# Modulation rows gathered in one accumulation bank per group of blocks, with twelve blocks in the opening

## The reference

```python
cond_lat = jax.nn.silu(c)[:, None, :]
cond_ctx = jax.nn.silu(c_ctx)[None, None, :]
for i in range(DEPTH):
    sh1, sc1, g1, sh2, sc2, g2 = jnp.split(cond_lat @ w_ada[i] + b_ada[i], 6, axis=-1)
    csh1, csc1, cg1, csh2, csc2, cg2 = jnp.split(cond_ctx @ w_ada[i] + b_ada[i], 6, axis=-1)
    h_lat = modulate(rms_norm(x, norm_gain[i, 0]), sh1, sc1)
    ...                                   # mixer: Fourier for i = 0, differential attention for i = 1
    x = x + g1 * o_lat
    x = x + g2 * swiglu(modulate(rms_norm(x, norm_gain[i, 1]), sh2, sc2), ffn_w_in[i], ffn_w_out[i])
```

## Time and profile before

| what | value |
|---|---|
| time, median of 3 runs | 2476.74 us (2475.94 to 2478.11) |
| profiled execution | 2477.43 us |
| its span, first to last instruction | 2475.3 us |
| PE busy | 2406.6 us, 97% of the span |
| DVE busy | 1295.9 us, 52% |
| ACT busy | 879.2 us, 36% |
| POOL busy | 374.7 us, 15% |
| granted PE clock, mean | 0.991 |

### The profile page before, as it was taken

One profiled execution on the slowest core, in us unless ns is written; L12 is line 12 of the kernel. 1 busy time (PEld: TensorE's weight loads), 2 busy tenths in 40 slices (PEclk: granted clock), 3 DMA queues, 4 the chain that ended last, 5 costly groups with the idle time before them and its releaser, 6 DMA issues.

```text
span 2475.3 us, 34693 instructions
## 1 busy us (share of the span) xinstructions
PE 2406.6 (97%) x14346; PEld 2015.3 (81%) x14346; DVE 1295.9 (52%) x2101; ACT 879.2 (36%) x1499; POOL 374.7 (15%) x301
## 2 busy tenths in 40 slices
PE   8999999999999999999999999999999999999999
PEld 6778888888887777656888887988989878877788
DVE  3765635543535776775333336465565445554433
ACT  4332111211224544434222124454544334444422
POOL 0210000000014444501000001234333410000000
PEclk9999999999999999999999999999999999999999
DMA  9734334334311111012333332222122121121222
GB/s 324 206 97 120 121 111 126 120 119 119 107 64 35 51 52 35 35 51 69 98 90 102 99 89 87 67 69 65 56 69 86 52 69 52 52 69 52 79 92 111
DMA packets 252744, 220.79 MB, mean 89 GB/s; under 512 B 7480, under 2 KB 243443, under 8 KB 252204
## 3 DMA queue, kind: packets, MB, share of 16 engines
q1 hardware_dynamic: 249072, 217.92, 28.6%
q10 hardware_dynamic: 3260, 0.58, 0.1%
q0 software_dynamic: 256, 0.07, 0.0%
HBM read 214.26 MB, written 6.29 MB: 89 GB/s over the span
## 4 chain that ended last, share of the span: by engine, by line
PE 60%; ACT 3%; DVE 3%; issue 2%; POOL 1%; DVEq 0%; ACTq 0%; POOLq 0%
PE two L685 10%; PE bank L1354 5%; PE bank L1545 4%; PE bank L685 4%; PE bank L1350 3%; PE bank L1331 3%; PE two L1285 3%; PE bank L1526 2%; PE bank L1051 2%; PE two L1156 2%; PE bank L1182 2%; PE two L1565 2%; PE bank L1021 1%; PE bank L1033 1%; PE two L1443 1%
## 5 line engine op out<-in xcount | busy, mean ns | idle before, releaser
L2560 DVE TENSOR_TENSOR wL<-ring,wH 128x512 fp32r<-128x512 f32 x224 | 182.9, 831 | 226.9 <-ACT wH L1832 226.7
L1823 ACT ACTIVATE wH<-ring 128x2048 fp32r<-128x2048 f32 (+1 forms) x80 | 149.1, 1864 | 272.1 <-PE bank L690 73.4
L2549 DVE TENSOR_TENSOR wL<-ring,wH 128x2048 fp32r<-128x2048 f32 (+1 forms) x80 | 179.0, 2237 | 82.2 <-ACT wH L1823 82.0
L685 PE MATMUL two<-h1H,wH 128*128 128x512 f32 x496 | 195.5, 394 | 0.0
L685 PE MATMUL two<-h1H,wL 128*128 128x512 f32 x496 | 193.5, 390 | 0.0
L685 PE MATMUL two<-h1L,wH 128*128 128x512 f32 x496 | 193.4, 390 | 0.0
L1832 ACT ACTIVATE wH<-ring 128x512 fp32r<-128x512 f32 x224 | 133.6, 623 | 60.3 <-PE bank L1331 22.5
L1901 ACT ACTIVATE gateS<-two 128x512 f32<-128x512 f32 x44 | 26.3, 598 | 330.5 <-PE bank L690 142.0
L2653 DVE SCALAR_TENSOR_TENSOR xT<-two,ada,xT 128x512 f32<-128x512 f32 (+1 forms) x48 | 30.6, 680 | 186.3 <-PE bank L690 66.3
L3196 POOL TENSOR_TENSOR rstd<-rstd,sq 128x768 f32<-128x768 f32 (+1 forms) x15 | 30.4, 2027 | 610.6 <-ACT sq L1859 609.6
L1354 PE MATMUL bank<-unH,wH 128*128 128x272 f32 (+1 forms) x368 | 111.9, 304 | 1.3 <-issue 0.8
(11 more groups left out here) (642 smaller groups left out, 6962.1 us busy)
## 6 DMA issues: line engine op xcount, KB each, us to landing
ring<-in_ffn_w_in SPq DMA_DIRECT2D x88, 512.0 KB, 5.2
ring<-in_w_in SPq DMA_DIRECT2D x40, 1024.0 KB, 5.0
ring<-in_w_ada SPq DMA_DIRECT2D x32, 1024.0 KB, 5.3
ring<-in_ffn_w_out SPq DMA_DIRECT2D x16, 1024.0 KB, 5.1
early<-in_w_ada SPq DMA_DIRECT2D x12, 1024.0 KB, 12.2
ring<-in_diff_w_in SPq DMA_DIRECT2D x12, 1024.0 KB, 5.2
ring<-in_w_proj_ssd SPq DMA_DIRECT2D x8, 1024.0 KB, 4.9
ring<-in_ffn_w_out SPq DMA_DIRECT2D x8, 768.0 KB, 4.6
```

Of the source, the lines that this page charges most:

```text
L685: m = nc.tensor.matmul(bank[3 * s + half], w, r[:, 0:LAT], start=i == 0, stop=i == n - 1)
L1823: nc.scalar.activation(hi, raw, ACT.Copy).then_inc(w_hi, 1)
L2549: nc.vector.tensor_tensor(lo, raw, hi.bitcast(F32), ALU.subtract).then_inc(w_lo, 1)
L2560: nc.vector.tensor_tensor(lo, raw, hi.bitcast(F32), ALU.subtract).then_inc(q_lo, 1)
```

## The change

The two ways become one. Blocks are gathered in six groups: blocks 0 to 7, blocks 8 to 11, and of the other 36 (`MORE`) numbers 0 to 7, 8 to 11, 12 to 27 and 28 to 35. All blocks of a group add into one bank: the weight tile is cut from a wider `condz` (62 columns, the two conditions in the middle), so that block j of a group lands in rows 2j and 2j + 1 of each strip. After the last block DVE copies the bank once (`sums_out`), PE collapses it with two products against a selector of 32 columns (`cols_of`), and DVE stores all columns of the group at once (`take_ada`). DVE no longer sums blocks. The opening has 12 blocks instead of 16, the Fourier tiles 8 instead of 4, the feed-forward 28 as before, one after each of units 1 to 28. The loads of the first two Fourier blocks go between the modulation loads, the first directly behind block 7; POOL folds all four, and the first split moves in ACT's and DVE's order.

```diff
-ADA0 = [4, 5, 6, 7, 0, 1, 2, 3] + list(range(8, FRONT))
+ADA0 = list(range(FRONT))
+UNITS0 = sum([[("in", 0, c) for c in range(lo, hi)] + [("down", 0, lo, cb) for cb in range(4)] for lo, hi in GROUPS], [])
+ADA_GROUPS = [[("ada", 0, b) for b in range(8)], [("ada", 0, b) for b in range(8, FRONT)], MORE[0:8], MORE[8:12], MORE[12:28], MORE[28:36]]
+ROWS_AT = {0: [0], 1: [1], 2: [2], 3: [3], 4: [4, 5], 5: [6], 6: [7]}
...
-    plan = [("ada", 0, b) for b in ADA0]
-    plan += [("fnet", 0), ("fnet", 1), ("fnet", 2), MORE[0], ("fnet", 3)] + MORE[1:4]
+    plan = [("ada", 0, b) for b in range(8)] + [("fnet", 0)] + [("ada", 0, b) for b in range(8, FRONT)]
+    plan += [("fnet", 1), ("fnet", 2), MORE[0], ("fnet", 3)] + MORE[1:8]
+    for u, unit in enumerate(UNITS0):
+        plan += [unit] + (MORE[6 + u:7 + u] if u >= 2 else [])
...
             sp.dma_start(wback[:, 0, :], w64raw[8:16, :]).then_inc(s_rev, 16)
-            for n in range(8, N_OF[("fnet", 0)]):
-                stream(n)
             sp.wait_ge(s_rev, 32)
             for n in range(N_OF[("fnet", 0)], len(PLAN)):
...
+            def rows_of(key):
+
+                w = slot(N_OF[key])
+                g = [key in group for group in ADA_GROUPS].index(True)
+                j, last = ADA_GROUPS[g].index(key), key == ADA_GROUPS[g][-1]
+                n = N_OF[key]
+                pe.wait_ge(ring_ready[slot_of(n)], arrived(n))
+                if j == 0 and g < 2:
                     pe.wait_ge(s_cols, 3)
+                elif j == 0:
+                    pe.wait_ge(ada_taken, g)
                 for kc in range(KC):
                     q = 32 * (kc % 4)
+                    m = nc.tensor.matmul(bank[(4, 5, 7, 6, 7, 6)[g]][q:q + 32, 0:256], condz[:, kc, 30 - 2 * j:62 - 2 * j], w[:, kc, :],
+                                         start=j == 0 and kc < 4, stop=last and kc >= 4)
                 m.then_inc(ada_row, 1)
...
+            def cols_of(g):
+
+                pe.wait_ge(ada_ev, g + 1)
                 for h in range(2):
+                    m = nc.tensor.matmul(bank[6 + g % 2 if g < 2 else 7 - g % 2][:, 256 + 32 * h:288 + 32 * h], adacc[:, g % 2, P * h:P * h + P], sel,
                                          start=True, stop=True)
                 m.then_inc(ada_done, 1)
...
             def more_columns(key):
+                u = UNITS0.index(key)
+                for g in (3, 4, 5):
+                    if u == MORE.index(ADA_GROUPS[g][-1]) - 6:
+                        cols_of(g)
+                if 1 <= u < len(MORE) - 7:
+                    rows_of(MORE[7 + u])
...
-                    pe.wait_ge(ada_taken, FRONT + 4)
+                    pe.wait_ge(ada_taken, 3)
...
                 for i in ([], [], [0], [1], [2, 3], [4], [5, 6], [7])[g]:
                     ada_rows(i)
-                    if i:
-                        ada_cols(i - 1)
-            ada_cols(7)
             for kc in range(4):
                 x_turned(kc)
-                ada_rows(8 + kc)
-                if kc:
-                    ada_cols(7 + kc)
+                if kc == 0:
+                    cols_of(0)
+                if kc < 2:
+                    ada_rows(8 + kc)
             for p in range(4):
                 dft_features(p)
-                ada_rows(12 + p)
-                ada_cols(11 + p)
+                if p in (1, 2):
+                    ada_rows(9 + p)
             dft_middle()
-            ada_cols(FRONT - 1)
+            cols_of(1)
...
-            keep_busy(4, 5)
+            keep_busy(2, 5)
...
+            cols_of(2)
...
+            for t in range(9):
+                if t == 5:
+                    split_hi(0)
...
+            def sums_out(g):
+
+                dve.wait_ge(ada_row, sum(len(x) for x in ADA_GROUPS[:g + 1]))
+                if g >= 2:
+                    dve.wait_ge(ada_done, g - 1)
+                nc.vector.tensor_copy(adacc[:, g % 2], bank[(4, 5, 7, 6, 7, 6)[g]][:, 0:256]).then_inc(ada_ev, 1)
...
             def more_sums(key):
+                u = UNITS0.index(key)
+                for g in (3, 4, 5):
+                    if u == MORE.index(ADA_GROUPS[g][-1]) - 7:
+                        sums_out(g)
+                    if u == MORE.index(ADA_GROUPS[g][-1]) - 6:
+                        take_ada(g)
...
             turned_lat(4)
             turned_lat(5)
-            folded_weights()
+            split_lo(0)
             turned_lat(6)
             turned_lat(7)
-            split_lo(0)
             split_lo(1)
...
                     mixed(m)
-                    for j in ROWS_AT.get(m, ()):
-                        strip_out(j)
-                    for j in COLS_AT.get(m, ()):
-                        take_ada(FRONT + j)
+                    if m == 6:
+                        sums_out(2)
                 split_lo(cb + NS)
+            take_ada(2)
             multipliers(1)
...
-            for cb in range(1, 4):
+            for cb in range(4):
                 n = N_OF[("fnet", cb)]
                 w = slot(n)
-                pool.wait_ge(w_sum, 2 * cb)
                 pool.wait_ge(ring_ready[slot_of(n)], arrived(n))
-                pool.wait_ge(w_lo, max(cb - 1, 1))
+                if cb == 0:
+                    pool.wait_ge(f_a, 2 * KC)
+                if cb >= 2:
+                    pool.wait_ge(w_lo, cb - 1)
```

More of the change, by code:

```diff
@@ L30 @@
 EARLY = 24
-FRONT = 16
+FRONT = 12
 NS = 2
@@ L61, in constants @@
         k[:, K_NYQ + 33 * j] = np.cos(a)[:, DH]
-    for c in range(2):
-        k[c::32, K_SEL + c] = 1.0
+    k[:, K_SEL:K_SEL + 32] = i[:, None] % 32 == i[None, 0:32]
     k[2, K_BIAS] = 1.0
@@ L139, in stream_plan @@
 def stream_plan():
-    plan = [("ada", 0, b) for b in ADA0]
-    plan += [("fnet", 0), ("fnet", 1), ("fnet", 2), MORE[0], ("fnet", 3)] + MORE[1:4]
+    plan = [("ada", 0, b) for b in range(8)] + [("fnet", 0)] + [("ada", 0, b) for b in range(8, FRONT)]
+    plan += [("fnet", 1), ("fnet", 2), MORE[0], ("fnet", 3)] + MORE[1:8]
+    for u, unit in enumerate(UNITS0):
+        plan += [unit] + (MORE[6 + u:7 + u] if u >= 2 else [])
     for layer in range(2):
[L144 to L151, removed]
+        if layer:
+            for lo, hi in GROUPS:
+                plan += [("in", 1, c) for c in range(lo, hi)] + [("down", 1, lo, cb) for cb in range(4)]
         if layer == 0:
@@ L714, in ada_rows @@
                 m.then_inc(ada_row, 1)
[L716 to L735, removed]
@@ L743, in strip_cols, with ada_rows @@
                 m.then_inc(ada_done, 1)
[L745 to L750, removed]
-                        o = 4 * h + 2 * c
-                        m = nc.tensor.matmul(bank[6 + j % 2][:, o:o + 2], adacc[:, j % 2, c, P * h:P * h + P], ones[:, 0:2],
-                                             start=True, stop=True)
-                m.then_inc(ada_done, 1)
+            def ada_rows(i):
+                rows_of(("ada", 0, i))
@@ L866, in _ @@
             for _ in range(11):
-                nc.tensor.matmul(bank[7][:, 0:256], condz[:, 0:4, :].rearrange("p c n -> p (c n)"), condz[:].rearrange("p c n -> p (c n)"),
-                                 start=True, stop=True)
+                zeros = condz[:].rearrange("p c n -> p (c n)")
+                nc.tensor.matmul(bank[7][:, 0:256], zeros[:, 0:P], zeros[:, 0:256], start=True, stop=True)
             for g in range(KC):
@@ L988, in _ @@
             ffn(0)
-            pe.wait_ge(ada_taken, 48)
+            pe.wait_ge(ada_taken, 6)
             norm_sums(2, True)
@@ L1768, in _ @@
             act.wait_ge(s_cols, 3)
-            for to in (condz, cond):
-                for j, r in enumerate((ROW_C, ROW_CC)):
-                    nc.scalar.activation(to[:, :, j], colA[:, r:r + 8], ACT.Silu).then_inc(s_cols, 1)
+            for j, r in enumerate((ROW_C, ROW_CC)):
+                nc.scalar.activation(condz[:, :, 30 + j], colA[:, r:r + 8], ACT.Silu).then_inc(s_cols, 1)
             nc.scalar.preload_act_table_set("natural_log_exp_and_others")
@@ new lines, in take_ada @@
+            def take_ada(g):
+                dve.wait_ge(ada_done, g + 1)
+                n, (_, layer, b) = len(ADA_GROUPS[g]), ADA_GROUPS[g][0]
+                src = bank[6 + g % 2 if g < 2 else 7 - g % 2][:, 256:320].rearrange("p (h m) -> p h m", h=2)[:, :, 0:2 * n]
+                src = src.rearrange("p h (j c) -> p j h c", c=2)
+                o = 48 * layer + 2 * b
+                bias = colB[:, o:o + 2 * n].rearrange("p (j h) -> p j h", h=2).unsqueeze(3).broadcast_to([P, n, 2, 2])
+                nc.vector.tensor_tensor(ada[layer][:, 2 * b:2 * b + 2 * n, :].rearrange("p (j h) c -> p j h c", h=2), src, bias, ALU.add) \
+                    .then_inc(ada_taken, 1)
@@ L2440, in more_sums @@
             def more_sums(key):
[L2442 removed]
+                if key not in UNITS0:
                     return
[L2444 to L2468 removed]
@@ L2470, in multipliers @@
+                u = UNITS0.index(key)
[4 more added lines that the diff above has]
+                        take_ada(g)
```

(5 more changed lines are left out.)

147 lines of the change are left out of this document (29 added, 118 removed).

## The result

The changed kernel takes 2508.0 us, median of 4 runs (2504.4 to 2514.2), against 2476.4 (2475.9 to 2478.1) for the kernel before: 1.0129 times as long, interval 1.0115 to 1.0143. It is slower, by 31.6 us; 23.8 were forecast. The median lies 1 us above the forecast range of 2489 to 2507.

The account below looks back on a forecast made before the run. TensorE was taken to bound layer 0's feed-forward, with a serial chain behind the opening. Terms -1.7 + 2.3 + 2.3 + 1.2 + 3.5 + 11.2 + 5.0 = 23.8 us on the 2476.74 median gave 2500.5, range 2489 to 2507.

Parts of the forecast that it names:

- The two stops: Feed-forward units 5 and 21: TensorE stands until VectorE takes the group before, 6.9 and 4.3 us, 11.2 lost.
- Rival D: Units 5 and 21: no stop, take done before PE asks or PE runs past; removes 16.2, leaves 7.6; chance 0.05.
- Half clock behind the stops: Feed-forward units 5 and 21: TensorE's clock at half after each stop, 2.5 us each, 5.0 lost (bounds 0 and 7).
- Blocks in the feed-forward stage: Layer 0's feed-forward: 28 wide blocks on TensorE replace 9 blocks and 19 DVE-summed ones, 34.7 for 31.2, 3.5 us lost.
- Fourier tiles and hand-over: Fourier tiles: eight blocks for four, 2.3 us lost; hand-over to the norm: take behind a weight split, another 2.3 lost.
- Half clock at the norm: Before the norm sums: the hole growing to 3.1 us may halve TensorE's clock, 1.7 if it comes, 1.2 taken.
- The opening: Up to the first Fourier tile: start at 96.0 instead of 97.66, 1.7 us won (bounds 3.9 won, 0.9 lost).
- Rival B: Opening: loads run at stream rate once released, block 8 at 61.2, first tile at 88.2, total 2492.7 us; chance 0.14.
- Rival C: Opening held longer by half clock or later Fourier weights: first tile at 98.5 to 101, total 2503 to 2506; chance 0.08.
- Everything behind it is one chain, so the sum needs four pieces: Whole kernel: only opening, Fourier tiles, hand-over to the norm and the 34 feed-forward units were counted.

Follow-up runs that it names:

- e1: Changed kernel with the first block of groups 4 and 5 waiting for the take one group earlier; 2494.5 us, ratio to the kernel before 1.0071.
- e8: Changed kernel with looser stops, earlier second take, blocks 8 to 11 before the Fourier weights, ScalarE's split back, four fillers and both pads; 2478.0 us, ratio 0.9998.
- e5: Changed kernel with 64 unused bytes a partition ahead of cond alone; 2502.3 us, one execution.
- e6: Changed kernel with 1088 unused bytes a partition behind condz alone; 2496.6 us, one execution.
- e3: Changed kernel with the second group's columns taken behind token tile 7's step, before the weight block's split; 2506.1 us.
- e2: Changed kernel with two unused tiles (64 and 1088 bytes) putting ring, weights, h1 and hid back at their old addresses; 2496.5 us, ratio to the kernel before 1.0084.
- e12: Kernel before the change with 512 unused bytes a partition behind condz; 2473.1 us, one execution.
- e10: Kernel before the change with 960 unused bytes a partition behind condz; 2494.5 us, ratio to the unpadded kernel 1.0071.
- e4: Changed kernel with blocks 8 to 11 issued before SP waits for the scratch copy, the first Fourier weights behind them; 2505.9 us, ratio to the kernel before 1.0123.
- e7: Changed kernel with e4's load order and ScalarE's first split moved back behind the last turned tile; 2507.3 us, ratio to the kernel before 1.0123.
- e9: e8 with VectorE's first low split moved behind its last two turned chunks; 2473.4 us, ratio to the kernel before 0.9979.
- e11: Kernel before the change with 960 unused bytes a partition ahead of the ring, distances kept; 2479.8 us, one execution.

## Why the prediction was right and wrong

The direction, the mechanism and, within 1.7 us or the scatter, the sizes of its seven terms held. The term by which it missed wasn't in the sum.

**The two stops** (11.2 forecast): 6.90 and 4.34, 11.24. e1 takes them away and wins 13.5 in the median with what the clock gives back. Rival D is refuted: TensorE does stand for the take. The rule of the Trainium skill cited against D ("TensorE: Matmul & The Clock Gate", "Step-by-step: what each phase is for") agrees: the products behind the waiting one stayed behind it, for 6.90 us.

**Half clock behind the stops** (5.0): it came at both, at 0.50 from 270.3 to 277.1 and from 563.9 to 570.6, but began inside the hole both times. So of 6.8 and 6.7 us TensorE worked only in 3.09 and 4.30, an estimate of 3.7 lost; e1 prices it at 3.3. Inside the bounds, 1.7 too high.

**Blocks in the feed-forward stage** (3.5): e8's 586.1 against 582.4 before, so 3.7. Right.

**Fourier tiles and hand-over** (2.3 and 2.3): from the first tile to the norm sums it was 48.7 before and 54.6 in the profiled execution, 53.0 in e5 and e6, whose clock didn't fall at the start of the tiles: 4.3 to 5.9 for 4.6. The hand-over alone, by e3, 2.2; the norm sums began 5.37 behind the last tile's end (5.4 forecast). **Half clock at the norm** (1.2): 1.7 in the profiled execution, none in e5; it comes in some executions, and in e3 without the hole.

**The opening** (-1.7): -1.4 in the profiled execution, -2.6 to -2.8 in e5 and e6. That the 96.0 met 96.24 so closely is in part luck: the features started 1.7 sooner than the 76 that the working had, and the first tile 22.0 behind them, not 19.4. The scatter is as large, too: with the changed kernel's order of loads and splits the tile starts between 93.87 (e3) and 96.47 (e2), with the old order between 96.78 (e12) and 99.09 (e10). Block 8 was waited for 10.92 (11 forecast), because it stood behind the Fourier weights in SP's queue. Rival B, loads at the stream's rate, is refuted for this pair: TensorE's wait ended at 65.66, 66.8 was forecast, and B said 61.2. The estimate by the Trainium skill's "DMA: Bandwidth & Descriptors" ("Anatomy of one DMA"), about 62, fell with B. Rival C, an opening held to 98.5 or longer, didn't come. A slip without effect stands in the working of the first stop: from 276.84 to 284.15 is 7.31, not 7.36.

**What failed** is the step "Everything behind it is one chain, so the sum needs four pieces". It takes for granted that what the change doesn't edit keeps its duration, and so puts layer 1's feed-forward stage at nothing. The change shrinks adacc and cond and widens condz, which shifts h1 and hid against the weights, and layer 1's feed-forward stage grew by 10.3. Added to the sum of 23.8 it gives 34.1 for the 31.6 that were measured. Where the 2.5 went isn't shown; the half clock at the stops, 1.7 less than forecast, is the largest known piece. The profiled execution alone is 37.1 longer in span: 24.9 in the parts that the seven terms cover, 10.3 in layer 1, 1.9 in the other stages. e2 (all places restored: -11.5), e6 (this shift alone undone: 359.6 in the stage), e10 (a shift of 960 bytes alone, on the kernel before: +16.0) show it as the cause. The diff told of the shift, in the three declarations; no row of before could price it.

The Trainium skill says of TensorE's reads ("SBUF — State Buffer", section "Who interferes with whom") that its two read ports, for moving operand and for weight loads, are independent and that it never waits on anyone. The runs don't fit this independence: with nothing changed but one pad between the two operands (e10), a 512-column product took 233.5 ns in place of 227.0. The measurement decides. By what mechanism the distance acts, and why the 256-column products get quicker by it (277 and 281 for 284), stays open; only the old distance and changes of 512, 960 and -1088 bytes were tried.

Where did the change's own gain go? It removed 152 records of narrow products of TensorE (19 blocks, 8 records each) and 335 instructions of VectorE in layer 0's feed-forward stage (515 to 180). VectorE's were never on the path, since TensorE was busy in all of the 582.4 us. TensorE's were replaced by wide blocks that cost 3.7 more. The opening's gain was held by one load and by three orders in queues: SP's (e4), ScalarE's (e7), VectorE's (e9). With all three, in e9, the first tile starts at 88.64, 9.0 sooner than before the change; VectorE's order without the other two wasn't tried.

## What to carry to other kernels

When a diff changes the size of a tile, list which later tiles move and by how much, and compare the mean duration of an untouched product (by shape) before and after; a pad of unused bytes tests it in one run. A wait that is written as "the group before" should be read as "which instruction of which queue ends it", and loosened to what the data need. Where a step is moved up on one engine, the same tile's steps on every other queue must be moved too, or the gain stops at the first queue left behind: here it stopped at ScalarE in e4 and at VectorE in e7.

## What the runs showed of the hardware

The step of a 512-column product depended on the distance between its operands in memory: 227.0 ns at the old distance (before, e2, e6, e11) and at 512 bytes more (e12), 233.5 ns at 960 more (e10) and at 1088 less (the changed kernel, e1, e5), the clock granted in full in all of them. It costs 10.3 us in a stage of 1584 products.

VectorE's subtraction of a 128x1024 split took 1.22 us alone (87.76 in e7, GpSimd idle) and 3.36 beside a fold on GpSimd (85.22 in e9; the fold runs from 84.29 to 87.50). The Trainium skill's "SBUF — State Buffer" ("Who interferes with whom") says that a VectorE instruction with two SBUF inputs contends with GpSimd's reads, and the row agrees. So moving the fold to GpSimd isn't free: in e9 this split is what the first tile waits for.

How often half clock comes differs between executions of the same instructions: the changed kernel took 2504.4 us with a mean granted clock of 0.990 and 2514.2 with 0.985, and e5, 64 bytes apart from it, 2502.3 with 0.993.
